# A decoder step's 64-token tile on TensorE by column halves, and the rows of 56 dots in PSUM

## The reference, cut to what matters

```
x += mixer(rmsnorm(x))        # w_in (1024 x 7168), short conv, spatial gate, w_a_out, w_b_out, w_mix_o
x += cross_attn(rmsnorm(x))   # 4 heads of 256 into 256 memory tokens; w_xq, w_xo; own keys and values per sample sequence
x += peer(rmsnorm(x))         # 8 heads, 128 experts a token picked out of 16384

# peer, for token t with expert indices idx[t, 0:128] and gates g[t, 0:128]
a[t, e] = gelu(dot(h[t], peer_u[idx[t, e]]))
out[t]  = sum over e of g[t, e] * a[t, e] * peer_v[idx[t, e]]
```

## Time and profile before

| what | value |
|---|---|
| median of 3 runs | 4169.25 us |
| the profiled execution's own time | 4173.51 us |
| its span | 4171.6 us |
| TensorE busy | 3355.2 us (80%) |
| VectorE busy | 2984.4 us (72%) |
| POOL busy | 2674.4 us (64%) |
| ACT busy | 950.2 us (23%) |
| read from HBM | 1512.62 MB |
| mean granted clock of TensorE | 0.917 |

### The profile page before, as it was taken

How to read it: one execution, slowest core, us unless ns; L and a number is a source line. 1 busy time by engine, 2 the same in 40 slices (tenths; PEclk the granted TensorE clock), 3 DMA queues, 4 the chain that set the end, 5 groups by cost and what they waited for, 6 DMA issues and landing times. The chain is left out here.

```text
span 4171.6 us, 36434 instructions
## 1 busy us (share of the span) xinstructions
PE 3355.2 (80%) x10976; PEld 2005.5 (48%) x10976; DVE 2984.4 (72%) x5971; ACT 950.2 (23%) x2770; POOL 2674.4 (64%) x2318
## 2 busy tenths in 40 slices
PE   9999989999889688866757969898878857755655
PEld 6866636665546235655334626664545422212211
DVE  2110679976767877887878789997867777676676
ACT  1001321121323322122113321121313222321211
POOL 0000485676657677787677676776856777777775
PEclk9999999999989999887878989899889999989878
DMA  6444799998999999999999989999999999999998
GB/s 220 141 149 152 306 353 367 385 402 340 403 348 403 373 354 406 402 404 406 410 406 402 406 302 400 404 404 406 359 405 377 400 409 407 409 411 410 409 410 337
DMA packets 462380, 1522.33 MB, mean 365 GB/s; under 512 B 41221, under 2 KB 45605, under 8 KB 462185
## 3 DMA queue, kind: packets, MB, share of 16 engines
q0 software_dynamic: 331776, 1208.11, 73.9%
q1 hardware_dynamic: 130408, 311.90, 19.9%
HBM read 1512.62 MB, written 7.23 MB: 364 GB/s over the span
## 5 line engine op out<-in xcount | busy, mean ns | idle before, releaser
L918 POOL DMA_INDIRECT urow<-in_peer_u_dram,idx x1152 | 1379.0, 1197 | 1069.7 <-DVE idx L1692 449.3
L918 POOL DMA_INDIRECT vrow<-in_peer_v_dram,idx x1152 | 1293.2, 1123 | 408.1 <-issue 325.4
L981 PE MATMUL ps<-vrow,diag 128*128 128x512 f32 x1900 | 996.4, 660 | 419.9 <-DMA vrow<-in_peer_v_dram,idx 365.2
L1006 PE MATMUL ps<-RH,W 128*128 128x256 f32 (+1 forms) x4608 | 1190.7, 420 | 124.8 <-DMA W<-in_w_in_dram 50.2
L1567 DVE CUSTOM_DVE_ANT_0 urow<-urow,T 128x1024 f32<-128x1024 f32 x768 | 937.3, 1223 | 247.8 <-DMA urow<-in_peer_u_dram,idx 197.7
L1006 PEld LDWEIGHTS ps<-RH,W 128*128 128x128 f32 x4608 | 907.1, 198 | 410.8 <-issue 98.2
L981 PEld LDWEIGHTS ps<-vrow,diag 128*128 128x128 f32 x1900 | 363.8, 206 | 1004.7 <-issue 836.8
L1583 DVE SCALAR_TENSOR_TENSOR X<-vrow,wts,X 128x1024 f32<-128x1024 f32 x598 | 769.2, 1286 | 108.0 <-issue 93.9
L1567 DVE CUSTOM_DVE_ANT_0 urow<-urow,ps 128x1024 f32<-128x1024 f32 x320 | 389.1, 1219 | 220.7 <-DMA urow<-in_peer_u_dram,idx 217.7
L1317 ACT ACTIVATE gel<-dots 128x4 f32<-128x4 f32 x288 | 59.1, 205 | 1975.0 <-DVE dots L1567 1949.5
L1006 PE MATMUL ps<-RB,W 128*128 128x256 f32 (+1 forms) x1024 | 258.4, 414 | 14.7 <-DMA W<-in_w_b_out_dram 5.6
(11 more groups left out here) (259 smaller groups left out, 2359.5 us busy)
## 6 DMA issues: line engine op xcount, KB each, us to landing
W<-in_w_in_dram SPq DMA_DIRECT2D x56, 2048.0 KB, 18.8
W<-in_w_pq_dram SPq DMA_DIRECT2D x16, 2048.0 KB, 18.6
urow<-in_peer_u_dram,idx POOLq DMA_INDIRECT x1152, 14.8
vrow<-in_peer_v_dram,idx POOLq DMA_INDIRECT x1152, 14.8
W<-in_w_a_out_dram SPq DMA_DIRECT2D x8, 2048.0 KB, 19.2
W<-in_w_b_out_dram SPq DMA_DIRECT2D x8, 2048.0 KB, 19.0
W<-in_w_mix_o_dram SPq DMA_DIRECT2D x8, 2048.0 KB, 14.1
W<-in_w_xq_dram SPq DMA_DIRECT2D x8, 2048.0 KB, 18.9
```

The lines of the kernel that those rows point to most:

```text
L918: return pool.indirect_dma_start(ring[:, slot, :], None, table, bass.IndirectOffsetOnAxis(ap=idx[:, q % TSLOT, e:e + 1], axis=0))
L981: o = pe.matmul(ps[:, bank + b, :], diag[:, pe_turn[m] % NDIAG, :], vrow[:, m % NV, b * 512:(b + 1) * 512], start=m in pe_first, stop=m in ...
L1006: m = pe.matmul(pf(name), slot(u)[:, k, c % BLK * P:c % BLK * P + P], src[:, k, 0:ncols(name[0] % 2)], start=(k == 0), stop=(k == KC - 1))
```

## The change

- Matmuls of the sample tile in "v", "mo", "xo", "ss" and "os" write two halves of one bank: output columns 0 to 511 (or heads 0 and 1) on partitions 0 to 63, the rest on partitions 64 to 127, one after the other in program order. Evacuations, softmax and transposes follow this layout; the tile's jobs take one bank (`wide`), and the cost of each "os" job is 2.5, not 3.5.
- All 64 picks of the sample tile are summed on TensorE in passes 1 and 3, with diagonals of 128 x 64 (two 64 x 64 activations) that add both halves of the partitions, and two matmuls onto the halves of one bank. `finish` only counts.
- Before pass 1, ACT copies the normalised rows of its first tile into banks 4 and 5 (`copy_beside`); the dots of its first 56 picks read them there. From 16 steps before to 56 steps after the start of pass 1, jobs get banks 0 to 3 only.

```diff
+ROWS_APART = 56
+    def wide(i):
+        return 2 if GROUPS[g][i][1] == P else 1
-    jobs += [(("v", i), "act", 2, tm(i, nt)) for i in range(nt)]
+    jobs += [(("v", i), "act", wide(i), tm(i, nt)) for i in range(nt)]
...
-        jobs += [(("os", b), "act" if b == NSEQ - 1 else "none", 2, 3.5) for b in range(NSEQ)]
+        jobs += [(("os", b), "act" if b == NSEQ - 1 else "none", 1, 2.5) for b in range(NSEQ)]
...
+def rows_apart(p, since, place):
+    base = step_base(1)
+    return p == 1 and place > base - 16 or p == 2 and since < base + ROWS_APART
...
-                top = 6 if held or summing else 8
+                top = 4 if rows_apart(p, since, place[k]) else 6 if held or summing else 8
...
-            span(b + n - CLOSE, b + n, step_base(p + 1) + LAG + 1, lambda m: p % 2 or m % 4)
+            span(b + n - (tile_picks(NS) if p % 2 else CLOSE), b + n, step_base(p + 1) + LAG + 1, lambda m: p % 2 or m % 4)
...
-            share = 2 if i == len(GROUPS[p % 2]) - 1 else 3
-            span(at, end, step_base(p) + end - b + LAG, lambda m: (m % share or not i and m >= b + CARRY) and m >= since)
+            span(at, end, step_base(p) + end - b + LAG, lambda m: (m % 3 or not i and m >= b + CARRY or rows < P) and m >= since)
...
+                if name in AFTER_ROWS:
+                    pe.wait_ge(u_read, step_base(1) + ROWS_APART)
...
                     for b in range(2):
-                        o = pe.matmul(ps[:, bank + b, :], diag[:, pe_turn[m] % NDIAG, :],
+                        out = ps[:, bank + b, :] if rows == P else ps[half_rows(b), bank, :]
+                        o = pe.matmul(out, diag[:, pe_turn[m] % NDIAG, 0:rows],
...
                             for a in range(2):
-                                m = pe.matmul(ps[0:rows, BANK[p, kind, i] + a, :], src[:, k, i * P:i * P + rows],
+                                out = ps[:, BANK[p, kind, i] + a, :] if rows == P else halves((p, kind, i))[half_rows(a), :]
+                                m = pe.matmul(out, src[:, k, i * P:i * P + rows],
...
-                    for h in range(HEADS):
+                    for j in range(2):
                         for e in range(2):
+                            for a in range(2):
+                                c = 2 * (2 * a + j) + e
+                                last = pe.matmul(out[half_rows(a), j * NMEM:(j + 1) * NMEM], qS[b][:, c, :], kbT[b % 2][:, c, :],
...
+            def copy_beside():
+                for name in LAST_APART:
+                    await_evac(act, name)
+                act.wait_ge(xn_done, norms_to(1, 2, 0))
+                act.activation(rows_beside, normed(tiles_to(1, 0) - 1), ACT.Copy).then_inc(rows_copied, 1)
...
+            asides += [(step_base(1) - 8, copy_beside, ())]
...
-                    act.activation(diag[:, pe_turn[m] % NDIAG, :], ident[:, :], ACT.Copy,
+                    for first in range(0, P, rows):
+                        part = slice(first, first + rows)
+                        made = act.activation(diag[part, pe_turn[m] % NDIAG, 0:rows], ident[part, part], ACT.Copy,
...
-                if rows < P:
-                    half = normed(q)[0:rows, :]
-                    ch.link(dve.tensor_copy(half, X[rows:P, t, :]))
-                    if not streams_last(q):
-                        ch.mark(dve.memset(X[rows:P, t, :], 0.0))
-                    ch.link(dve.tensor_tensor(X[0:rows, t, :], X[0:rows, t, :], half, ALU.add))
                 dve.sem_inc(x_final, 1)
...
+                    ch.link(dve.tensor_tensor(X[0:rows, t, half_cols(0)], X[0:rows, t, half_cols(0)], ps[half_rows(0), bank, :], ALU.add))
+                    total = dve.tensor_tensor(X[0:rows, t, half_cols(1)], X[0:rows, t, half_cols(1)], ps[half_rows(1), bank, :], ALU.add)
...
+                if reads_beside(m):
+                    if e == 0:
+                        dve.wait_ge(rows_copied, 1)
+                    rows = rows_beside
```

More of the change, by code:

```diff
@@ L168, in phase_jobs @@
         jobs += memory
-    jobs += [(("mo", i), "dve", 2, tm(i, nt)) for i in range(nt)]
+    jobs += [(("mo", i), "dve", wide(i), tm(i, nt)) for i in range(nt)]
     if not g:
@@ L201, in phase_jobs @@
         jobs += [(("fg",), "row", 2, 2)]
-    jobs += [(("xo", i), "dve", 2, tm(i, nt)) for i in range(nt)]
+    jobs += [(("xo", i), "dve", wide(i), tm(i, nt)) for i in range(nt)]
     norms = [(("n", 2, i), "act", 2, 2) for i in range(nt)]
@@ L563, in norm_rows, with reads_beside @@
             return (XN_APART if n and p % 2 else XN)[:, i, :]
+        def reads_beside(m):
+            q, e = picks[m]
+            return peer_tiles[q][0:2] == (1, 0) and e < ROWS_APART
         def streams_last(q):
@@ L583, in pf, with half_rows, half_cols, halves @@
             return ps[:, BANK[job], 0:ncols(job[0] % 2)]
+        def half_rows(a):
+            return slice(a * NS, (a + 1) * NS)
+        def half_cols(a):
+            return slice(a * 512, (a + 1) * 512)
+        def halves(job):
+            return ps[:, BANK[job], :]
         def pt(job, rows=P):
@@ L1148, in prob_transposes @@
                     pe.wait_ge(prob_done, tiles_to(p, i))
-                    transposes((p, "pt", i), [probs[i % 2][0:rows, j * P:(j + 1) * P] for j in range(8)], rows, P)
+                    transposes((p, "pt", i), [probs[i % 2][:, j * P:(j + 1) * P] for j in range(8 if rows == P else 4)], P, P)
                 def key_transposes(b):
@@ L1202, in trunk @@
                 if g:
-                    out = pt((p, "os", 0), NS)
+                    out = halves((p, "os", 0))
                     for b in range(NSEQ):
@@ L1207, in trunk @@
                         pe.wait_ge(ps_done, NSEQ * l + b + 1)
-                        for h in range(HEADS):
+                        for j in range(2):
                             for m in range(MC):
-                                last = pe.matmul(out[:, h * HD:(h + 1) * HD], pS[b][:, 2 * h + m, :],
-                                                 cached(p, "vb", b)[:, m, h * HD:(h + 1) * HD],
-                                                 start=(b == 0 and m == 0 and h % 2 == 0),
-                                                 stop=(b == NSEQ - 1 and m == MC - 1 and h % 2 == 1))
+                                for a in range(2):
+                                    h = 2 * a + j
+                                    last = pe.matmul(out[half_rows(a), j * HD:(j + 1) * HD], pS[b][:, 2 * (2 * j + m) + a, :],
+                                                     cached(p, "vb", b)[:, m, h * HD:(h + 1) * HD],
+                                                     start=(b == 0 and m == 0 and j == 0),
+                                                     stop=(b == NSEQ - 1 and m == MC - 1 and j == 1))
                         end(last)
                     await_evac(pe, (p, "os", NSEQ - 1))
-                    transposes((p, "ot"), [probs[0][0:NS, c * P:(c + 1) * P] for c in range(KC)], NS, P, NS)
+                    transposes((p, "ot"), [probs[0][:, c * P:(c + 1) * P] for c in range(KC // 2)], P, P)
                     await_evac(pe, (p, "ot"))
@@ L1390, in trunk @@
                     finished((p, "n", 0, nt - 1))
-                    act.activation(VT[0:rows, i, :], pt((p, "v", i), rows), ACT.Gelu_apprx_tanh).then_inc(act_evac, 1)
+                    if rows == P:
+                        gelu = act.activation(VT[:, i, :], pt((p, "v", i)), ACT.Gelu_apprx_tanh)
+                    else:
+                        ch.mark(act.activation(VT[0:rows, i, half_cols(0)], halves((p, "v", i))[half_rows(0), :], ACT.Gelu_apprx_tanh))
+                        ch.wait()
+                        gelu = act.activation(VT[0:rows, i, half_cols(1)], halves((p, "v", i))[half_rows(1), :], ACT.Gelu_apprx_tanh)
+                    gelu.then_inc(act_evac, 1)
                 act.wait_ge(ln_stat, tiles_to(p, nt - 1))
@@ L1454, in exps @@
                         finished((p, "pt", i - 2))
-                    for h in range(HEADS):
-                        e = act.activation(probs[i % 2][0:rows, h * NMEM:(h + 1) * NMEM],
-                                           pt(name, rows)[:, h * NMEM:(h + 1) * NMEM], ACT.Exp,
-                                           bias=nmax[0:rows, i, h:h + 1], scale=1.0 / 16.0,
-                                           accum_out=rsum[0:rows, i, h:h + 1])
+                    scores = pt(name) if rows == P else halves(name)
+                    for h in range(HEADS if rows == P else HEADS // 2):
+                        e = act.activation(probs[i % 2][:, h * NMEM:(h + 1) * NMEM],
+                                           scores[:, h * NMEM:(h + 1) * NMEM], ACT.Exp,
+                                           bias=nmax[:, i, h:h + 1], scale=1.0 / 16.0,
+                                           accum_out=rsum[:, i, h:h + 1])
                     e.then_inc(act_evac, 1)
@@ L1853, in add_to_x @@
                     take((p, kind, i))
```

(8 more changed lines are left out.)

47 lines of the change are left out of this document (28 added, 19 removed).

## The result

The changed kernel takes 4124.98 us (median of 4 runs, 4123.31 to 4129.31), against 4171.32 us before (median of 4, 4165.64 to 4175.3): ratio 0.9886, 95% interval 0.9872 to 0.9900. The forecast was 31 us less; 46 us came.

A forecast was written before the change was run, and what follows sets the result against it. The stream of picks was taken as DMA-bound at 409 GB/s, losing 156 us where disturbed. Terms 12 + 9 + 4 + 3 + 3 = 31 us off 4173.5 gave 4142.5, 4138 for the median; whole range 4110 to 4168.

The forecast's parts named there:

- Pairs halve TensorE's time: Sample tile's matmuls in trunks: two halves overlap, saving 101 us of TensorE, 51 us a pass.
- Late trunk, pass 0: Around 1190 us, VectorE waits for "fg" and "xo" (32 us); pairs take back 9 of 16.8 us lost.
- between 0 and 5 us each way: Pairs in "v" and "mo", beside a busy VectorE: counted as nothing, with these bounds.
- Pass 2: Around 3150 us, pairs shorten the wait for "xo": 4 of 7.7 us; near 2460 us, 3 us more.
- Fewer back-to-back operations: I take 3 us: Around 2460 us, VectorE sheds sums and the finish ahead of a starved call losing 19 us; bounds 0 and 15.
- Rows beside: Pass 1's first 56 dots read rows from PSUM, so gather calls shorten: 12 us, bounds 5 and 20.
- End of pass 1: All 64 sample picks summed on a full TensorE: in pairs 63 us, for 110 us of 56 picks before.
- The end: After the last sum's matmuls: shorter matmuls, merge and add in halves; 3 us less.
- Pairs that don't overlap: Rival: sample tile's paired matmuls save nothing, late trunk stays, pass 1's end gets more matmul; 4167 us, chance 0.13.
- Starved calls coming back: Rival: the new order of due steps makes one or two more long gather calls; 4155 to 4172 us, chance 0.14.
- Drains at tile switches: Rival: at pass 1's end TensorE drains switching between 128 and 64 columns; 4209 us, chance 0.04.
- More than forecast: Rival: both late-trunk holes and the 19 us around 2480 us vanish whole; 4110 us, within the forecast's tail.

The follow-up runs named there:

- e10: Changed kernel with no matmul pairs left that can overlap, in trunk or sums, against the kernel before: 4302.85 us for 4297.00, ratio 1.0012 (chip 10).
- e5: The changed kernel itself against the kernel before, on chip 0: 4253.25 us for 4271.83, ratio 0.9962.
- e12: The changed kernel itself against the kernel before, on chip 15: 4255.75 us for 4276.98, ratio 0.9945.
- e4: Changed kernel with only the sample tile's sums unpaired, against the kernel before: 4282.82 us for 4296.64, ratio 0.9972 (chip 15).

## Why the prediction was right, and where it wasn't

The direction, the mechanisms and the range (4110 to 4168) held; the forecast of 4138 was 13 us too slow.

- **Pairs halve TensorE's time.** Right: 1.94 times for projections. For "ss" and "os" too much was promised: 24 us each saved over both passes, not 29 and 30. For the sums too: 64 picks in pairs keep TensorE busy for 80.5 us in pass 1, not 63, and for 105.7 us in pass 3, at a lower clock. As the prediction said, the DMA of the values of "os" is late next.
- **Late trunk, pass 0: 9 us forecast for the hole, 19.0 measured over the pass.** By the dots, 5.3 us were gained up to pick 168, 13.4 between picks 168 and 200, where the hole was, and 0.3 after. Two things in the term for the hole were mis-sized. I took back about half of the 16.8 us lost there, because 25 us of saved path stood against 32 us of waits; the waits were 49.6 us with the one ahead of "ss", of which 14.8 are left. And what was left (8.55 and 4.53 us) cost almost nothing, at 396 GB/s: 35 us less wait gave 13.4 us, so a wait doesn't cost the stream in proportion. How long a wait the row buffers cover wasn't measured. The 5.3 us ahead of the hole stand against "between 0 and 5 us each way" for "v" and "mo". VectorE's waits ahead of "mo" fell from 7.34, 10.21 and 11.50 us to 4.88, 8.58 and 8.03, but picks 128 to 168 took 165.7 us, 166.5 before, so nothing of the gain lies beside them; where the 5.3 us come from isn't shown.
- **Pass 2: 4 for "xo" and 3 for the start, 7.9 measured.** Picks 168 to 208, with "fg" and "xo", gave 4.8 us, near the 4 forecast; VectorE's waits there fell from 11.32 and 10.71 us to 2.61 and 2.15. The start gave nothing (206 GB/s). "Fewer back-to-back operations: I take 3 us" failed: the sums that left VectorE lie ahead of the run of dots which starves the calls there, and that run is unchanged. Another 5.1 us were gained by pick 168 and 2.0 lost after pick 208, which no term has; dots of the two traces wander by some 4 us against each other, so that the sum fits is in part luck.
- **Rows beside: 12 forecast, 16.7 measured** on the first chip, by the two traces. The deduction for the top-k and the boundary (21.5 cut to 12) was too large. The signs that the prediction named are there: calls of 1031 and 959 ns, and from 1380 us on

```profile
1380.00:1520.00 140.00, 114.50 (x263) 46.06 (x263) 114.67 (x333) 39.02 (x128) 107.21 (x108) 0.98 1.02 404
```

- **End of pass 1.** Pairs were needed only to keep this stretch where it was: with 64 picks on TensorE they make 100.00 of 100 us into 75.81, and the rest of pass 1 moved by -0.8 us. What the move to TensorE would have cost without them shows in e10 alone, 22 to 29 us more than in e5 and e12 for the rest of pass 1; e4's 9 to 17 us lie within what the other kernels scatter.
- **The end: 3 forecast, 2.7 measured.** Right, step by step.
- **The rivals.** Pairs that don't overlap: fell by the first trace, and e10 shows the price that it gave (no gain, "4167"). Starved calls coming back: two over 10 us, one less than before, only because the third now comes in pieces of 9.65 and 7.31 us; no new one came, and the rival fell. Drains at tile switches: 64 picks switch back and forth in pass 1, and the stretch is no longer. The rival fell as a cost; TensorE has 24 us of idle time in 100 there, so by this alone a short drain could be hidden. "More than forecast", both trunk holes gone: the trunk half of it is what happened; its third part, the 19 us at the start of pass 2, did not.

The sum by the terms that were measured is 19.0 + 16.7 + 0.8 + 7.9 + 0.3 + 2.7 + 1.3 = 48.7 us of spans, 4171.6 - 4122.9. The 31 us of the forecast fell short by 10 us in pass 0 and by 5 us in the first 56 picks; the 1.3 us ahead of the first dot are in a part that the change doesn't touch.

## What to carry to other kernels

Don't count a saved wait in proportion when there are buffers behind it: here what was left of the waits cost almost nothing. Before pricing them, add up all waits of the stretch, not the longest two. If half-width matmuls are issued in neighbouring pairs on two halves of the output partitions, their TensorE time nearly halves, and it is the order of issue, not the placement, that does it; then look for the DMA that was hidden behind them, and look at the granted clock. A stalled queue isn't lost time by itself: before removing a stall, look for the next wait behind it that will take up what is gained. And when two traces are compared by picks, move the boundary by a few picks and see whether the difference stays.

## What the runs showed of the hardware that was not expected

**Gathers alone run at different rates on different chips.** 409 GB/s at a DMA share of 1.03 on the first chip, 367 at 0.96 on chip 15 and 372 at 0.98 on chip 0 (500 us of pass 3, same kernel). With the trunk's weights in the mix (1600 to 2300 us) they reach 404, 405 and 402. Pass 3 takes 905.9 and 911.4 us in e5 and e12 against 830.4, which is three fifths of the 122 and 126 us by which the spans of those executions are longer. On such a chip the shorter gather calls bring nothing that shows; on the first one their stretch is 16.7 us shorter.

**One indirect-gather call can be starved through a whole run of VectorE instructions.** 17.81 us beside 23 VectorE instructions, mostly dots and sums that read two operands from SBUF, none longer than 1.3 us; a VectorE wait for its own last result, some 0.1 us between a dot and a sum, ends it. The Trainium skill ("SBUF — State Buffer", "SBUF: two separate sides") says that the loser of the shared port is blocked for the whole instruction of the other; here a call was held for 17.81 us, over many instructions that followed one another back to back. With one operand in PSUM (the dots of the first 56 picks) calls take 1031 and 959 ns instead of 1315 and 1061.

**Pairs of half-width matmuls gave half the time only at the higher clock.** Four paired matmuls of a pick take 1.08 us in pass 1 and mostly 1.97 us in pass 3, where the mean granted clock is 0.65 from 4000 to 4100 us. TensorE was busy for 67.55 of those 100 us; with the pairs undone (e4, 4100 to 4200 us) it was busy for 72.71 and granted 0.95. So the pairs relieved it by little there: 105.7 us for 64 picks, 127.3 undone.
